# The second layer norm's scale and bias move behind the gather, and two freed buffers take the first expert's weights

## The reference, cut to what matters

```
def layer_norm(x, g, b):
    ...
    y = (x32 - mu) * lax.rsqrt(var + LN_EPS)
    return (y * g.astype(jnp.float32) + b.astype(jnp.float32)).astype(x.dtype)

def moe_ffn(x, w_router, b_router, w_gate_up, b_gate_up, w_down, b_down):
    logits = (xt @ w_router + b_router).astype(jnp.float32)
    top_val, top_idx = lax.top_k(logits, TOP_K)
    gates = jax.nn.softmax(top_val, axis=-1)
    ...
        h = xb @ w_gate_up[e] + b_gate_up[e]
        g, u = h[:, :D_EXPERT], h[:, D_EXPERT:]
        ...
        return ((u + 1.0) * glu) @ w_down[e] + b_down[e]

        x = layer_norm(DEEPNORM_ALPHA * x + h, ln2_g[l], ln2_b[l])
        h = moe_ffn(x, w_router[l], b_router[l], w_gate_up[l], b_gate_up[l],
                    w_down[l], b_down[l])
        x = layer_norm(DEEPNORM_ALPHA * x + h, ln3_g[l], ln3_b[l])
```

## Time and profile before

| | us |
|---|---|
| median of three runs (1204.78 to 1205.69) | 1204.81 |
| span of the profiled execution, first to last instruction | 1202.1 |
| PE busy, of the span | 1146.8 |
| ACT, DVE and POOL busy | 133.3, 219.4, 49.7 |

### The profile page before, as it was taken

The page is one execution under the profiler, slowest core; times in us unless marked ns, Lnnn a source line. Parts: engine busy times, 40 slices in busy tenths (PEclk is TensorE's granted clock), DMA queues, the critical chain, the costliest instruction groups (busy, mean ns, idle before and its releaser), DMA issues.

```text
span 1202.1 us, 12962 instructions
## 1 busy us (share of the span) xinstructions
PE 1146.8 (95%) x5354; PEld 522.3 (43%) x5354; DVE 219.4 (18%) x559; ACT 133.3 (11%) x281; POOL 49.7 (4%) x56
## 2 busy tenths in 40 slices
PE   9999999999999999999999999898989899999986
PEld 7686747754434343433434343333333333333322
DVE  1232122224211111121111111111111111111113
ACT  2133111222100000010000000000000000000001
POOL 0232002010000000000000000000000000000001
PEclk9999999999999999999999999999999999999998
DMA  9953334398999999999999999999999999999995
GB/s 350 323 204 141 133 112 157 122 373 326 429 429 427 427 414 429 428 429 430 427 429 427 427 428 429 429 430 427 428 428 430 429 429 427 429 430 429 427 429 215
DMA packets 55698, 446.63 MB, mean 372 GB/s; under 512 B 10304, under 2 KB 11472, under 8 KB 30192
## 3 DMA queue, kind: packets, MB, share of 16 engines
q1 hardware_dynamic: 53200, 440.49, 88.3%
q10 hardware_dynamic: 2464, 5.66, 1.3%
HBM read 445.06 MB, written 1.07 MB: 371 GB/s over the span
## 4 chain that ended last, share of the span: by engine, by line
PE 62%; DMA 35%; DVE 2%; issue 1%; SPq 0%; ACT 0%
DMA ring<-in_w_gate_up 32%; PE bank L1693 21%; PE bank L1333 9%; PE bank L1742 9%; PE bank L1320 8%; DMA ring<-in_w_down 3%; PE bank L1577 3%; PE bank L1638 2%; PE bank L1653 1%; PE bank L1367 1%; PE bank L1718 1%; PE bank L1792 1%; PE bank L1731 1%; PE bank L1519 1%; PE bank L1497 1%
## 5 line engine op out<-in xcount | busy, mean ns | idle before, releaser
L1693 PE MATMUL bank<-ring,PT 128*64 128x512 f32 x1792 | 396.5, 594 | 29.9 <-DMA ring<-in_w_gate_up 29.9
L1693 PEld LDWEIGHTS bank<-ring,PT 128*64 128x64 f32 x1792 | 125.9, 137 | 295.3 <-issue 235.4
L1182 DVE TENSOR_SCALAR reg_k<-bank 128x512 f32<-128x512 f32 x32 | 22.1, 691 | 449.9 <-PE bank L1693 444.1
L1320 PE MATMUL bank<-reg_bc,ring 128*128 128x256 f32 x448 | 99.6, 381 | 0.0
L805 ACT ACTIVATE reg_v<-reg_k 128x512 f32<-128x512 f32 x30 | 18.9, 630 | 689.3 <-DVE reg_k L1182 689.3
L1742 PE MATMUL bank<-reg_q,NCt 128*64 128x512 f32 x400 | 92.0, 602 | 0.0
L1320 PEld LDWEIGHTS bank<-reg_bc,ring 128*128 128x128 f32 x448 | 84.4, 190 | 14.1 <-issue 3.2
L1742 PE MATMUL bank<-reg_bc,NCt 128*64 128x512 f32 x400 | 90.1, 592 | 0.0
L1577 PEld LDWEIGHTS bank<-L,reg_a 128*128 128x128 f32 x512 | 62.9, 196 | 24.8 <-issue 23.5
L1577 PE MATMUL bank<-L,reg_a 128*128 128x128 f32 x512 | 69.3, 288 | 1.0 <-DVE L L1096 0.7
L1213 DVE COPY reg_v<-bank 128x512 f32<-128x512 f32 x28 | 19.4, 692 | 269.0 <-PE bank L1742 269.0
(11 more groups left out here) (232 smaller groups left out, 709.0 us busy)
## 6 DMA issues: line engine op xcount, KB each, us to landing
ring<-in_w_gate_up SPq DMA_DIRECT2D x114, 2048.0 KB, 23.3
reg_bc<-in_w_down SPq DMA_DIRECT2D x26, 2048.0 KB, 20.7
reg_q<-in_w_down SPq DMA_DIRECT2D x25, 2048.0 KB, 19.2
ring<-in_w_down SPq DMA_DIRECT2D x8, 2048.0 KB, 18.9
ring<-in_w_in SPq DMA_DIRECT2D x5, 2048.0 KB, 17.1
reg_kv<-in_w_gate_up SPq DMA_DIRECT2D x5, 2048.0 KB, 18.0
ring<-in_w_down SPq DMA_DIRECT2D x9, 1024.0 KB, 7.3
reg_q<-in_w_gate_up SPq DMA_DIRECT2D x4, 2048.0 KB, 14.2
```

The lines of the kernel that those rows point to most:

```text
L1182: nc.vector.tensor_scalar(gbuf, banks[0][:, :], LIMIT, None, ALU.min).then_inc(g_ready, 1)
L1320: last = mm(B(name)[:, a * T:(a + 1) * T], w[:, k, c:c + P], src[:, k, :], start=(k == 0), stop=(k == KD - 1))
L1693: last = mm(ps[half * CAP:(half + 1) * CAP, :], xgT[:, k, i * CAP:(i + 1) * CAP], w[:, j, col:col + HALF], start=(opens and k == 0), stop= ...
```

## The change

The gather takes normalised tokens without scale and bias (`x2hat`, in reg_v in the place of x1). The scale and bias of the second norm come as two columns for each of eight feature blocks (`lncol` 4 and 5), and ACT applies them when it copies gathered columns: four instructions of 128 columns for each half in the place of one of 512. POOL's and DVE's passes over x2 fall away, and so do the two loads of rows. The residual is put together in pair 6: matmuls of a matrix of ones with diagonals (`diag`, made by POOL in x_nat) spread the scale over the partitions and add the bias, DVE multiplies the scale with x2hat, and PE adds the products to the sums.

SP's queue changes with it. Expert 0's first chunk goes into x_nat and reg_a (1 MB each, `lent[0]` and `lent[1]`), which are free long before the first expert; reg_k takes half of its second chunk (`lent[2]`), and `OPENING` loses its first entry. The first gate and up product goes through the rows in the order 4, 5, 6, 7, 3, 2, 0, 1, with the right half of the gathered columns first. The third norm's rows are loaded behind the last weights.

The diff, cut to its core:

```
             for n, slot in enumerate(ORDER):
...
                 if n == 0:
                     load_half(0, 1, slot_in[0])
-                    load_half(NSLOT, 0, ahead_in)
+                    load_half(NSLOT, 0, ahead_in[0])
+                    wait_evacuated(sp, ("wo1", 1))
+                    load_lent(0, (0, 0), lent_in[0])
+                    sp.wait_ge(ln_out, TT)
+                    load_lent(1, (0, 0), lent_in[1])
                     continue
                 if n == NSLOT - 1:
-                    sp.dma_start(lent, chunk_source(0, 0)[:, 0:1, :]).then_inc(lent_in, 16)
+                    load_lent(2, (0, 1), lent_in[2])
                 load_chunk(*OPENING[n], n)
-            sp.wait_ge(gained2, 2)
-            sp.wait_ge(gained2_dve, 2)
-            sp.dma_start(lng[2], ln3_g.to_broadcast([P, D])).then_inc(ln_in[2], 16)
...
             def evac_xgT(half, m):
                 act.wait_ge((xgTa_done, xgTb_done)[half], m)
-                nc.scalar.activation(xgT[:, 4 * half:4 * half + 4, :],
-                                     (xy_ps, tr_ps)[half][:, :].rearrange("p (k c) -> p k c", k=4),
-                                     ACT.Copy).then_inc((xgTa_sb, xgTb_sb)[half], 1)
-
+                for j in range(4):
+                    k = 4 * half + j
+                    last = nc.scalar.activation(xgT[:, k, :], (xy_ps, tr_ps)[half][:, j * P:(j + 1) * P], ACT.Identity,
+                                                scale=lncol[:, 4, k:k + 1], bias=lncol[:, 5, k:k + 1])
+                last.then_inc((xgTa_sb, xgTb_sb)[half], 1)
+
+            act.wait_ge(lncol2_in, 32)
+            evac_xgT(1, 1)
             evac_xgT(0, 1)
-            evac_xgT(1, 1)
...
+            def scaled_residual():
+
+                dve.wait_ge(h_ready, 2 * BASE_PAIR + 1)
+                for half in range(2):
+                    cols = slice(half * HALF, (half + 1) * HALF)
+                    dve.wait_ge(gain_done, half + 1)
+                    if half > 0:
+                        dve.wait_ge(scaled_used, half)
+                    for tt in range(TT):
+                        last = nc.vector.tensor_tensor(scaled_x2[tt], xy_ps[:, :], x2hat[:, tt, cols], ALU.mult)
+                    last.then_inc(scaled_ready, 1)
...
             def base(p):
 
+                pe.wait_ge(diag_ready, 1)
+                pe.wait_ge(y_sb, p * 2)
+                for half in range(2):
+                    rows = slice(4 * half, 4 * half + 4)
+                    if half > 0:
+                        pe.wait_ge(scaled_ready, half)
+                    mm(xy_ps[:, :], one, diag[:, 0, rows, :].rearrange("p k f -> p (k f)"),
+                       start=True, stop=True).then_inc(gain_done, 1)
+                    for tt in range(TT):
+                        mm(acc[tt][half][:, :], one, diag[:, 1, rows, :].rearrange("p k f -> p (k f)"),
+                           start=False, stop=False, skip_group_check=True)
+                    pe.wait_ge(scaled_ready, half + 1)
+                    for tt in range(TT):
+                        last = mm(acc[tt][half][:, :], ident, scaled_x2[tt], start=False, stop=False, skip_group_check=True)
+                    last.then_inc(scaled_used, 1)
                 pe.wait_ge(rep_ready, 1)
-                pe.wait_ge(y_sb, p * 2)
                 for j in range(2):
...
-                for tt in range(TT):
-                    for half in range(2):
-                        mm(acc[tt][half][:, :], K[:, C_AID:C_AID + P], x2[:, tt, half * HALF:(half + 1) * HALF],
-                           start=False, stop=False, skip_group_check=True)
                 pe.wait_ge(cand_ready, 1)
```

More of the change, by code:

```diff
@@ L613, in _ @@
             last.then_inc(gw_ready, 1)
[L614 to L617, removed]
-                nc.gpsimd.tensor_tensor(x2[:, tt, cols], x2[:, tt, cols], lng[1][:, cols], ALU.mult).then_inc(gained2, 1)
-                pool.wait_ge(gained2, n + 1)
-                nc.gpsimd.tensor_tensor(x2[:, tt, cols], x2[:, tt, cols], lnb[1][:, cols], ALU.add).then_inc(x2_pool, 1)
             wait_filled(pool, ("rpart", 1))
             nc.gpsimd.memset(bdn, 0.0).then_inc(moe_zeroed, 1)
+            pool.wait_ge(gu_done, 1)
+            for i in range(2):
+                last = nc.gpsimd.tensor_tensor(
+                    diag[:, i, :, :], K[:, C_AID:C_AID + P].rearrange("p (k f) -> p k f", k=1).to_broadcast([P, KD, P]),
+                    lncol[:, 2 + i, :].rearrange("p (k f) -> p k f", f=1).to_broadcast([P, KD, P]), ALU.mult)
+            last.then_inc(diag_ready, 1)
             pool.wait_ge(ln_in[2], 32)
@@ L769, in normalise @@
                 act.wait_ge(nmr_ready, tt + 1)
-                nc.scalar.activation(x2[:, tt, cols], x1[:, tt, cols], ACT.Identity, scale=rstd[:, 1, tt, 1:2],
-                                     bias=nmr[:, tt:tt + 1]).then_inc(xn_ready, 1)
+                wait_filled(act, ("rT", tt, half))
+                nc.scalar.activation(x2hat[:, tt, cols], x1[:, tt, cols], ACT.Identity, scale=rstd[:, 1, tt, 1:2],
+                                     bias=nmr[:, tt:tt + 1]).then_inc(x2hat_ready, 1)
             def four(name):
@@ L783, in _ @@
             nc.scalar.activation(warm[:, 2:3], K[:, C_EPS:C_EPS + 1], ACT.Exp)
+            for half in range(2):
+                normalise(1, half)
             act.wait_ge(ntop_ready, 1)
@@ L1595, in _ @@
             pe.wait_ge(s_tile0_ready, 1)
-            pe.wait_ge(x2_pool, 2)
-            gather(0, (0,))
+            pe.wait_ge(x2hat_ready, 2)
+            gather(1, (0,))
             router_part(1, 1)
             router(1)
-            gather(1, (0,))
+            gather(0, (0,))
             def base(p):
+                pe.wait_ge(diag_ready, 1)
+                pe.wait_ge(y_sb, p * 2)
+                for half in range(2):
+                    rows = slice(4 * half, 4 * half + 4)
[10 more added lines that the diff above has]
+                    last.then_inc(scaled_used, 1)
                 pe.wait_ge(rep_ready, 1)
-                pe.wait_ge(y_sb, p * 2)
                 for j in range(2):
@@ L1671, in chunk @@
                     n = FINAL[i, c]
-                    loads = OPEN * 2 * CH // NSLOT + 1
+                    loads = len(range(n, len(OPENING), NSLOT)) + 1
                     if n < CH:
```

137 lines of the change are left out of this document (60 added, 77 removed).

## The result

The median of five runs is 1209.36 us (1209.13 to 1210.15), against 1204.81 us of five runs of before (1204.48 to 1206.67): 4.55 us more, a ratio of 1.004 with a 95% interval of 1.0028 to 1.0051. The forecast was 1209.3 us. The profiled execution had a time of 1209.23 us and a span of 1207.1 us. What lies around a span was 2.1 to 2.3 us in the five runs of after and 1.8 to 2.0 us in every run of before beside the experiments. The 2.7 us taken for it above hold some 0.8 us by which the profiled execution of before was faster than the median of its runs.

The account below looks back on a forecast made before the run. PE's pace to the 448 us issue, then the weight stream, was taken as the bound. Loads 0, start and copies 1.2, residual 3.3 sum to 4.5 us: span 1206.6 plus 2.7 gives 1209.3 us, range 1205.2 to 1212.0.

Parts of the forecast that it names:

- What bounds the kernel: PE's work from 285 to 448 us sets when SP may issue; the weight stream behind that issue sets the end.
- The loads, 0: Weights loaded earlier or later gain 0, against 7.3 us if the queue never ran dry; third norm's rows stay hidden.
- PE's start, 0.2 us: First gate and up product starts 0.2 us later; bounds 0.5 us earlier to 0.4 us later.
- The copies in pairs 1 and 2, 1.2 us: ACT's four-piece copies delay hT and down by 0.6 us in each pair, 1.2 us ahead of 448 us; bounds 0 to 1.6.
- The residual, 7.2 us of PE: Pair 6: 5.2 us of added passes plus 2.0 us waiting for cand; 3.3 us reach the end.
- The slack of 3.9 us: At the issue of 641.12 us behind pair 6's residual: 11.5 us to landing less 7.6 for an empty queue.
- The slack's rule: Slack is landing time less an empty queue's: 7.6 us from the trace for 2 MB, against 6.8 from the skill's fit.
- The loads did not count: Rival that loads count: stream gets and stays 7.3 us ahead, decided at the 448 us issue; 1197.5 us, chance 0.07.
- the residual did not stay hidden: Rival of a hidden residual: at most 1 us of it gets through in pair 6; 1205 to 1207.2 us, chance 0.21.
- The clock's second fall: Rival: PE's clock falls once more around pair 6's residual, costing 1 us or more; 1210.5 to 1212.5 us, chance 0.14.

Follow-up runs that it names:

- 12 MB less ahead of that issue: Kernel after with only the first half of each chunk of experts 4 and 5 loaded: 1209.52 us, 4.78 above before.
- nine places alone: Kernel after with nine places for weights during the first six pairs instead of three: 1210.24 us, 5.50 above before.
- the split too: Kernel after with residual in pair 6, tables in pair 8, and nine places for weights during the first six pairs: 1203.91 us, 1.04 below before.
- single copies: Kernel after with gathered tokens copied by one 512-column instruction per half, without scale and bias: 1208.50 us, 4.16 above before.
- DVE pieces: Kernel after with residual in pair 6, tables in pair 8, and DVE scaling half the gathered tokens from pair 1: 1204.74 us, 0.21 below before.
- the split: Kernel after with the residual kept in pair 6 and the tables moved to pair 8: 1205.98 us, 1.24 above before.
- the detour in pair 12: Residual and the tables behind it moved from pair 6 to 12, in after: 1209.27 us; in after with single copies: 1208.73 us.

## Why the prediction was right, step by step

**What bounds the kernel: right.** PE's pace up to 448 us, then the queue from each dry issue on. 12 MB less ahead of that issue changed nothing, while 3.3 us came back when the second dry issue was filled.

**The loads, 0: right, for the reason given.** At 341 us the stream was 2.0 us ahead of before (a landing at 341.24 against 343.27 us), not 7.3: the queue had been dry at 302.45 and 333.49 us as well. At 440 us 1.0 us of it was left, at 448 us nothing. With nine places alone the lead was lost in pair 6; with the split too 2.2 us were there at 520 us, and none from 800 us on. One reading was wrong without harm: the last weights of before land at 1186.86 us, not at 1177, so the third norm's rows, which land at 1195.39 us in after and are first used at 1199.93, had 4.5 us to spare and not some 12.

**PE's start, 0.2 us: 0.31 measured,** inside its bounds. From the first gather to the first product it is 3.07 us against 2.58.

**The copies in pairs 1 and 2, 1.2 us: 1.33 measured,** and both undoings, single copies and DVE pieces, give 114.82 us again. By the medians it is 1.45 us (split against split with DVE pieces). Start and copies together are what the split has left, 1.24 us above before in the medians; in its profiled execution the late landings behind pair 8 and the shorter end are in that as well.

**The residual, 7.2 us of PE: 7.23 measured.** The slack of 3.9 us took its part: the landing behind the detour is 5.07 us later than before, of which 1.68 were there already, so 3.39 against 3.3. By the medians it is 3.31 (4.55 less 1.24). In the rows another 0.9 us follow: two landings of after come late (5.86 us behind the one ahead at 668.45 us, 5.30 at 688.42, instead of 4.9), one of before (5.38 at 658.02). So the residual cost 4.26 us at PE's end, against 3.3 forecast; the forecast's slack counts only up to the first landing.

**What the sum left out, and luck.** In the profiled execution of after, against that of before, PE's end is 5.94 us later, of which start and copies are 1.68 (1.36 at 448 us) and the residual 4.26. Then 1.02 us go off behind PE's end, and 0.3 come on around the span: 5.2 us, against 4.5 forecast and 4.55 in the medians. The forecast had nothing for the late landings, the end or what lies around the span. The end is the change's and not one execution's: it took 9.6 us in the profiled executions of all eleven kernels with the change and 10.3 to 10.7 in the three without. In these three a transfer of 8 KB of the kind `instruction` (queue q14 of the page) starts between the issue and the landing of the last store, which takes 3.4 to 3.7 us; in the eleven it starts behind that landing, and the store takes 2.7. No experiment moves that transfer, so the cause is not shown. That the medians met the forecast to 0.05 us is luck: what was left out nearly cancels, and the median of before lay some 0.8 us above its profiled execution. The steps and their sizes are not luck.

**The slack's rule.** Five issues into a dry queue (449.63, 650.04, 651.15, 651.42 and 1004.51 us, in four kernels) landed in 7.5 to 7.8 us; at the place of 448 us two more with a hole ahead of them took 7.9 and 8.2 us (449.77 and 447.52 us, the two changed kernels with the detour in pair 12). The fit of the Trainium skill (DMA: Bandwidth & Descriptors, Anatomy of one DMA — SWDGE (gpsimd) path), 6.8 us for 2 MB as an estimate from that page, would have given a sum of 2.8 us by its slacks (the prediction has 2.9), 1207.6 us. The fit is for transfers on GpSimd's path, and these are SP's; for them the measurement decides against it.

**The rivals.** The loads did not count, and the residual did not stay hidden. The clock's second fall is real, though it is not in the profiled execution of after: it was there in the profiled executions of four of the seven kernels that hold the whole detour of the change in one pair, at 1.7 to 1.8 us each, above the 1 us or more of the forecast. Its chance of 0.14 was too low for this family of kernels. In after itself the mean granted clock of the runs speaks against it: 0.996 to 0.997 in all five, where the profiled executions of this family had 0.996 to 0.997 with one fall and 0.994 to 0.995 with two.

## What to carry to other kernels

Where transfers are issued as places come free, look for each issue that finds the queue dry, and count PE's work only as far as the next of them: a lead won ahead of a dry issue is lost there, and work that is added in front of one is paid in full beyond its slack. The slack is read from the issue that waits behind the added work (its time from issue to landing, less that of an empty queue), not from the last one ahead of it. Work that exceeds the slack in one place can lie under the transfers when it is cut in two and the parts stand where the lead has grown back. And a forecast that fits to a few hundredths may still have left out terms that cancel: sum the trace from one end to the other before calling it right.

## What the runs showed of the hardware

- Four ACTIVATE of 128 columns took 1.50 us against 0.60 for one of 512; DVE did four TENSOR_SCALAR of 128 columns from the same kind of source in 1.37 us, against 0.69 for one of 512 (L1182 of before). The pieces cost ACT 2.5 times and DVE twice the time.
- Behind an issue at 448 us or in the detour that found the queue dry, or nearly, one of the next three transfers landed 5.2 to 6.4 us behind the one ahead of it instead of 4.9 (5.64 at 471.36 us in before, 6.12 at 473.20 and 5.86 at 668.45 us in after), so the first landing shows the hole too small, by 1.2 and 1.0 us in after. The bytes were lost ahead of that: between 657 and 669 us after moves 431 GB/s.
- Such late landings are not peculiar to dry issues. The fourteen profiled executions have 48 of them (over 5.2 us, between 300 and 1180 us, with the queue not empty; the stretch of halved chunks left out), some in streams that were 20 us and more ahead. In each of the 48 a transfer of 16 KB of the kind `instruction` (queue q8 of the page), about 1.0 us long, had started at most 6.3 us before the landing, though such stretches of 6.3 us make up about a tenth of the time. What the two have to do with each other no experiment shows.
- PE's clock fell to 0.50 for 3.4 us at a time in the tables, once or twice from kernel to kernel with the same instructions around it. In after the fall stood on the transposes, bias products and first down products behind the tables; where a first one came earlier, the eight products of `bdn` took 5.37 us instead of 3.68.
